# One row of loads and one woven stretch for the first two expert units

## The reference, cut to what matters

```python
logits = (x @ w_router).astype(jnp.float32)
top_v, top_i = lax.top_k(logits, TOP_K)              # 2 of 8 experts for each token
gates = jax.nn.softmax(top_v, axis=-1)
combine = jnp.sum(jax.nn.one_hot(top_i, N_EXPERTS) * gates[..., None], axis=1)
for e in range(N_EXPERTS):
    out = out + combine[:, e:e + 1] * _swiglu(x, w_gate[e], w_up[e], w_down[e])
```

## Time and profile before

| | |
|---|---|
| Median of 3 runs | 1327.22 us (1326.99 to 1327.36) |
| The profiled execution | 1327.16 us, its span 1325.4 us |
| PE, DVE, ACT busy | 1279.3, 795.5, 642.1 us |
| Bytes moved, mean rate | 425.55 MB, 321 GB/s over the span |
| Issues on SP's queue | 422.67 MB |

### The profile page before, as it was taken

The page is one execution under the profiler, slowest core; times in us unless marked ns, Lnnn a source line. Parts: engine busy times, 40 slices in busy tenths (PEclk is TensorE's granted clock), DMA queues, the critical chain, the costliest instruction groups (busy, mean ns, idle before and its releaser), DMA issues.

```text
span 1325.4 us, 19510 instructions
## 1 busy us (share of the span) xinstructions
PE 1279.3 (97%) x7976; PEld 985.7 (74%) x7976; DVE 795.5 (60%) x977; ACT 642.1 (48%) x675; POOL 4.5 (0%) x12
## 2 busy tenths in 40 slices
PE   8999999999999999999769999999999999999996
PEld 8999999999999977885448885347887345888332
DVE  7564765653888679973129883118886215888122
ACT  7655644352576586761037772017774005776002
POOL 0000000000000000000000000000000000000000
PEclk9999999999999999999889999999999999999998
DMA  7335354463333498899999999999999999999995
GB/s 300 134 128 190 128 191 159 159 221 138 116 144 128 163 383 325 338 385 400 426 426 426 426 427 427 427 398 427 427 426 427 427 406 425 427 427 427 426 427 231
DMA packets 72351, 425.55 MB, mean 321 GB/s; under 512 B 6385, under 2 KB 8433, under 8 KB 27329
## 3 DMA queue, kind: packets, MB, share of 16 engines
q1 hardware_dynamic: 71680, 422.67, 78.6%
q0 software_dynamic: 432, 1.54, 0.3%
q10 hardware_dynamic: 144, 0.02, 0.0%
HBM read 423.16 MB, written 1.05 MB: 320 GB/s over the span
## 4 chain that ended last, share of the span: by engine, by line
PE 81%; DVE 8%; DMA 5%; ACT 3%; issue 3%; SPq 0%; DVEq 0%; ACTq 0%
PE ps L2436 11%; PE ps L2297 8%; PE ps L2298 7%; PE ps L2303 7%; PE ps L2468 6%; PE ps L1752 5%; PE ps L1742 4%; PE ps L1743 4%; PE ps L2322 4%; PE ps L2323 4%; PE ps L2330 4%; DMA unsplit<-in_moe_w_up 2%; PE ps L1790 2%; PE ps L1791 2%; PE ps L1807 2%
## 5 line engine op out<-in xcount | busy, mean ns | idle before, releaser
L1402 DVE TENSOR_TENSOR wl<-raw,wh 128x2048 fp32r<-128x2048 f32 x96 | 218.4, 2288 | 23.7 <-ACT wh L866 23.6
L866 ACT CAST wh<-raw 128x2048 fp32r<-128x2048 f32 x96 | 183.9, 1916 | 66.1 <-PE ps L2298 39.3
L2297 PE MATMUL ps<-wh,gh 128*128 128x512 f32 x448 | 176.3, 394 | 4.1 <-ACT wh L866 3.4
L2298 PE MATMUL ps<-wh,gl 128*128 128x512 f32 x448 | 175.4, 392 | 0.0
L937 ACT ACTIVATE sil<-ps 64x512 f32<-64x512 f32 (+1 forms) x28 | 15.0, 536 | 291.3 <-PE ps L2438 225.1
L2303 PE MATMUL ps<-wl,gh 128*128 128x512 f32 x448 | 120.4, 391 | 0.0
L1626 DVE COPY few_act<-ps 128x256 f32<-128x256 f32 (+1 forms) x28 | 11.0, 391 | 175.2 <-PE ps L2450 175.2
L1066 DVE TENSOR_TENSOR wl<-raw,wh 128x4096 fp32r<-128x4096 f32 (+1 forms) x18 | 73.2, 4069 | 61.7 <-ACT wh L625 39.7
L625 ACT CAST wh<-raw 128x4096 fp32r<-128x4096 f32 (+2 forms) x29 | 92.0, 3173 | 34.5 <-PE ps L1743 34.1
L2297 PEld LDWEIGHTS ps<-wh,gh 128*128 128x128 f32 x448 | 84.6, 189 | 23.9 <-issue 5.5
L2303 PEld LDWEIGHTS ps<-wl,gh 128*128 128x128 f32 x448 | 84.6, 189 | 17.9 <-DVE wl L1402 0.2
(11 more groups left out here) (365 smaller groups left out, 2672.0 us busy)
## 6 DMA issues: line engine op xcount, KB each, us to landing
raw<-in_moe_w_up SPq DMA_DIRECT2D x71, 1024.0 KB, 14.2
raw<-in_moe_w_gate SPq DMA_DIRECT2D x70, 1024.0 KB, 12.9
raw<-in_moe_w_down SPq DMA_DIRECT2D x51, 1024.0 KB, 14.5
unsplit<-in_moe_w_down SPq DMA_DIRECT2D x33, 1024.0 KB, 11.9
unsplit<-in_moe_w_up SPq DMA_DIRECT2D x25, 1024.0 KB, 14.4
unsplit<-in_moe_w_gate SPq DMA_DIRECT2D x22, 1024.0 KB, 19.1
raw_more<-in_moe_w_down SPq DMA_DIRECT2D x15, 1024.0 KB, 12.0
raw<-in_diff_w_qkv SPq DMA_DIRECT2D x8, 1536.0 KB, 6.6
```

The source lines that it names most:

```text
L866: act.copy(split_piece(wh, p), raw_piece(p, first)).then_inc(wh_ready, 1)
L1402: dve.tensor_tensor(split_piece(wl, p), raw_piece(p, first), raw_f(split_piece(wh, p)), ALU.subtract).then_inc(wl_ready, 1)
L2297: pe.matmul(ps[:, bank, :], gh[:, s], w, start=(k0 + k == 0), stop=False)
L2298: ins = pe.matmul(ps[:, bank, :], gl[:, s], w, start=False, stop=False)
```

## The change

1. The loads of the first wide unit and of the tiny unit become one list (`first_pair`) of 84 pieces. Place q mod 11 is taken by entry q, so both share eleven places and the six lent ones are not used in this pair. The list begins with 24 wide pieces; then come 4 tiny, 6 wide, 6 tiny, 6 wide, 6 tiny, 6 wide, and then the other 26 tiny ones.
2. PE weaves: after chunk i of the wide unit, for i = 3 to 6, it runs one share of the tiny unit (`tiny_share(i - 3)`): the transposition of the tiny chunk before, gate and up of the tiny chunk, down of the one before. The last three tiny chunks follow the wide unit (`tiny_rest`).
3. The tiny unit gets banks 5 (gate and up) and 6 (down) and buffers in `xn`; `gather` for the next unit goes to banks 0 and 1, both halves after chunk 5.
4. The routing on DVE is earlier: sort at j = 0, count at 1, list at 2, `save_tokens(3)` at j = 3 (it was at 1), `pick_pair(0)` at 5. PE's `gather_few(0)` and `turn_picks(0)` come after chunk 2. `turn(0)` waits for three saved tiles, and `down` of chunk 0 for the fourth.
5. `gather_few(1)` and `turn_picks(1)` come after the loop of `tiny_rest`, before the last two tiny down pieces.

```diff
+        def few_share(t):
+            return [("few", p) for p in range(few_up_at(t), few_up_at(t) + (6 if t else 4))]
+        def first_pair():
+            chunk = [CPU * 2 * c // FC - 2 if c else 0 for c in range(FC)] + [PIECES - 2, PIECES]
+            order = [("wide", p) for p in range(chunk[TINY_LAG])]
+            for t in range(FC - TINY_LAG):
+                order += [("wide", p) for p in range(chunk[t + TINY_LAG] + (2 if t else 0), chunk[t + TINY_LAG + 1] + 2)]
+                order += few_share(t)
+            for t in range(FC - TINY_LAG, FC):
+                order += few_share(t)
+            return order + [("few", p) for p in range(PIECES - 2, PIECES)]
...
+            def load_pair():
+                e = 0
+                for q, (kind, p) in enumerate(pair):
+                    s = q % RAW_SLOTS
+                    if q >= RAW_SLOTS:
+                        before, of = pair[q - RAW_SLOTS]
+                        if before == "wide":
+                            sp.wait_ge(wl_ready, C_MOE + of + 1)
+                        else:
+                            sp.wait_ge(few_used, of + 1)
...
+                    if p == 0:
+                        sp.wait_ge(routed, 1)
+                        e = expert(SMALL_UNITS[0])
...
-            load_wide(0, 0, first=True)
-            sp.wait_ge(routed, 1)
+            load_pair()
```

On ACT:

```diff
+            def tiny_rest():
+                for i in range(FC - TINY_LAG, FC):
+                    few_silu(0, i)
+                    if i == 5:
+                        gathered_high(2, unit=1)
+                few_tokens(1)
+                turned_picks(1)
...
                 for j, (kind, i) in enumerate(unit_chunks):
+                    if first and (kind, i) == ("g", TINY_LAG):
+                        few_tokens(0)
+                        turned_picks(0)
+                    if first and kind == "g" and i > TINY_LAG:
+                        few_silu(0, i - TINY_LAG - 1)
```

On DVE:

```diff
+            def tiny_rest():
+                wide_out(0)
+                few_turned_out(0, FC - TINY_LAG - 1)
+                dve.wait_ge(pick_turned, 1)
+                pick_pair(2)
+                dve.memset(bm["y"][:], 0.0)
+                for i in range(FC - TINY_LAG, FC):
+                    few_product(0, i)
+                    if i < FC - 1:
+                        add_wide(0, i - (FC - TINY_LAG))
+                    few_turned_out(0, i)
+                    if i == 5:
+                        gathered_low(2, unit=1)
...
+                    if first and kind == "g" and i > TINY_LAG:
+                        few_product(0, i - TINY_LAG - 1)
...
+                    if first and kind == "d" and TINY_LAG <= i < FC - 1:
+                        few_turned_out(0, i - TINY_LAG)
                     if 2 * j + 4 < PIECES:
                         unit_split(a, 2 * j + 4, first)
-                    if first and j < 2:
-                        save_tokens(2 + j)
+                    if first and j == 0:
+                        save_tokens(2)
+                        sort_experts()
+                    if first and j == 1:
+                        count_units()
                     if first and j == 2:
-                        sort_experts()
+                        list_units()
                     if first and j == 3:
-                        count_units()
-                    if first and j == 4:
-                        list_units()
+                        save_tokens(3)
+                    if first and j == 5:
+                        dve.wait_ge(gathered, 2)
+                        pick_pair(0)
...
-                    if first and j == 9:
-                        dve.wait_ge(gathered, 2)
-                        pick_pair(0)
```

On PE:

```diff
+            def few_turn(f, i):
+                pe.wait_ge(few_prod, f * FC + i + 1)
+                if i:
+                    pe.wait_ge(few_act_ready, f * FC + i)
+                if f == TINY_AT:
+                    pe.wait_ge(eal_ready, min(i + TINY_LAG + 2, FC))
...
+            def tiny_share(t):
+                if t:
+                    few_turn(0, t - 1)
+                few_up(0, t, 0)
+                few_up(0, t, 1)
+                if t:
+                    few_down(0, t - 1, 0)
+                    few_down(0, t - 1, 1)
+            def tiny_rest():
+                for i in range(FC - TINY_LAG, FC):
+                    few_up(0, i, 0)
+                    few_turn(0, i - 1)
+                    few_up(0, i, 1)
+                    few_down(0, i - 1, 0)
...
+                    if i in (4, 5):
+                        scatter_wide(0, i - 4)
+                    if i == 5:
+                        pe.wait_ge(pick_of, 2)
+                        gather(0, 1)
+                        gather(1, 1)
+                gather_few(1)
+                turn_picks(1)
+                few_down(0, FC - 1, 0)
+                few_down(0, FC - 1, 1)
...
                     pe.wait_ge(eal_ready, a * FC + i + 1)
+                    if first and i == 0:
+                        pe.wait_ge(acc_ev, 4)
...
                     elif first:
-                        pe.wait_ge(acc_ev, 4)
+                        pe.wait_ge(acc_ev, 3)
+                    if first and i > TINY_LAG + 1:
+                        pe.wait_ge(few_act_ready, i - TINY_LAG - 1)
...
-                    if first and i == 5:
+                    if first and i == TINY_LAG - 1:
                         gather_few(0)
                         turn_picks(0)
+                    if first and i >= TINY_LAG:
+                        tiny_share(i - TINY_LAG)
```

More of the change, by code:

```diff
@@ L528, in load_wide @@
+            def load_wide(a, e, few=None):
+                for p, (s, n) in enumerate(WIDE_PLACES):
                     kind, i = unit_chunks[p // 2]
                     if n:
[L531 to L542, removed]
+                        sp.wait_ge(wl_ready, a * PIECES + C_MOE + last_at(WIDE_PLACES[:p], s) + 1)
@@ L995, in _ @@
                 output_out(f)
-                few_body(u, f)
+                if f:
+                    few_body(u, f)
+                else:
+                    tiny_rest()
                 if u < LAST:
@@ new lines, in few_turn @@
+            def few_turn(f, i):
+                pe.wait_ge(few_prod, f * FC + i + 1)
+                if i:
+                    pe.wait_ge(few_act_ready, f * FC + i)
+                if f == TINY_AT:
+                    pe.wait_ge(eal_ready, min(i + TINY_LAG + 2, FC))
+                for k in range(few_cols(f) // P):
+                    s = slice(k * P, (k + 1) * P)
+                    ins = pe.transpose(ps[:, 4, s], few_prod_of(f)[:, s], ident)
+                ins.then_inc(few_turned, 1)
@@ new lines, in few_down @@
+            def few_down(f, i, half):
+                p = few_down_at(i) + half
+                if half == 0:
+                    pe.wait_ge(few_act_ready, f * FC + i + 1)
+                    if i == 0 and f:
+                        pe.wait_ge(wide_low, 2 * f + 2)
+                pe.wait_ge(*few_in(f + 1, f, p))
+                for k in range(2):
+                    held_, n = held(f), few_cols(f)
+                    to = slice((half * 2 + k) * held_, (half * 2 + k + 1) * held_)
+                    first_, last_ = i == 0 and half == 0 and k == 0, i == FC - 1 and half == 1 and k == 1
+                    for h in range(D // n):
+                        s = slice(k * D + h * n, k * D + (h + 1) * n)
+                        ins = pe.matmul(ps[h * held_:(h + 1) * held_, few_out_bank(f), 0:n], bm["few_act"][:, i % 2, to],
+                                        few_piece(f, p)[:, s], start=first_, stop=last_, skip_group_check=True)
+                ins.then_inc(few_used, 1)
@@ new lines, in few_body @@
+            def few_body(u, f):
+                few_up(f, 0, 0)
+                few_up(f, 0, 1)
+                for i in range(1, FC):
+                    few_up(f, i, 0)
+                    few_turn(f, i - 1)
+                    few_up(f, i, 1)
+                    few_down(f, i - 1, 0)
+                    if i == FC - 1:
+                        few_turn(f, i)
+                    few_down(f, i - 1, 1)
+                    before_ = 8 * f - 4
+                    if i in (1, 2):
+                        scatter_wide(f, i - 1)
+                    if i in (3, 4):
+                        scatter_few(f - 1, i - 3, (3, 7), before_ + 2 + 2 * (i - 3))
+                    if u < LAST and i in (3, 4):
+                        if i == 3:
+                            pe.wait_ge(pick_of, f + 2)
+                        gather(i - 3)
+                    if u < LAST and i == 5:
+                        gather_few(f + 1)
+                    if u < LAST and i == 6:
+                        turn_picks(f + 1)
+                few_down(f, FC - 1, 0)
+                few_down(f, FC - 1, 1)
```

252 lines of the change are left out of this document (126 added, 126 removed).

## The result

The changed kernel takes 1330.03 us (median of 14 runs, 1329.12 to 1331.25) against 1327.51 us (14 runs on the same chips, 1325.82 to 1329.69): ratio 1.0019, 95% interval 1.0011 to 1.0027, so 2.5 us slower. The forecast was 1328.5. The profiled execution took 1330.08 us with a span of 1328.2, 2.9 more than the one before.

A forecast was written before the change was run, and what follows sets the result against it. Weight transfers were taken to bound the kernel from slice 19 (630 us). Recovered idle transfers -6.7 plus a dense stream starting 8.0 us late gave +1.3 us, 1328.5; the forecast's own range was 1325.5 to 1332.

The forecast's parts named there:

- What bounds: Transfers bound from slice 19 (630 us); the landing of load 85, about 686, sets the next wide unit's start.
- Joining the lists: Loads of both units: tiny pieces fill SP's waits, the stream is dense from load 35 on, 6.7 us come back.
- The late saved tile: PE before down of chunk 0: stands still from 503.3 to 512.3, 9 us, waiting for DVE's last saved tile.
- The clock: PE behind the 9 us wait: slow clock costs 2.3 us; bounds 0 and 4.6 if two pieces run slow.
- PE dense from 512 on, SP's issues: First wide unit: piece 21 used at 557.9, loads 33 to 35 issued at 554.7, 557.5, 559.7; dense stream 8.0 us late.
- The woven stretch costs nothing: Shares among wide chunks: no cost if the stream stays fed; tightest at share 1, with three loads under way, 7.4 us.
- Rival C: Woven shares: PE waits 5.0 us a share for silu, product, cast and subtraction; 4.3 us paid, 1332.8; chance 0.17.
- A, filling alone: Dense stream's start: no PE wait, load 35 about 1 us late, idle transfers recovered, 1321.5; chance 0.18.
- B, the clock staying up: PE behind the saved-tile wait: the wait is there but no slow clock, -1.0 us, 1326.2; chance 0.15.
- `gather_few(1)` in the tail: End of tiny unit: gather, picks and two down pieces done at 687.3 against PE's next start at 689.3, two microseconds of cover.

The follow-up runs named there:

- filled gap: Changed kernel plus 20 unread matmuls of 256 columns on PE before the wait for the fourth saved tile: 1326.92 us, ratio 0.9993.
- lead of two: Two wide pieces loaded ahead of each share's tiny ones; taken out of the kernel with the routing at its old steps: 1339.84 us, ratio 1.0085.
- the kernel without the lead and with the turned tile first: Kernel without the two-wide-piece lead, with ACT and DVE taking the turned tile out ahead of piece 2j+3 in d3 to d5: 1332.53 us, ratio 1.0042.

## Why the prediction was right, and where its sizes were off

The experiments make a path from the kernel before to the changed one: gather early +2.5, row and weave -7.5, early routing +1.2, late saved tile +6.4 (1.0019 against 0.9971). They are differences of ratios, each uncertain by about 2 us, and they add up to the measured 2.5 by construction, so the sum proves nothing. On another path the parts would differ: the stall at turn 2 that goes with the early gather is not in the changed kernel, whose turn 2 starts at 534.31 without a wait.

The time was forecast at +1.3 and measured at +2.5. The terms were -6.7 + 8.0 and measured -6.4 + 10.3 = +3.9 at load 85. That the time is closer to the forecast than this is luck: the microsecond that comes back between load 85 and the end of the span (3.9 there, 2.9 here), most of it near 880, stands nowhere in the prediction, and no experiment was made on it.

*What bounds.* Right. The next wide unit is started by a transfer in both traces, 3.5 us later in the changed kernel, and the added PE work at share 2 cost nothing.

*Joining the lists.* Right in size: 6.7 forecast, 6.4 come back. The prediction gave all of it to the joined lists, though; with the gather early and the lists as before, 2.6 of them had come back already.

*The late saved tile.* Right: PE idle from 503.3 to 512.3 forecast, 8.78 us ending at 512.60 measured, released by DVE's copy, with DVE full meanwhile. Taking the wait away gave 5.6 us and adding it to the kernel before cost 5.4 by the ratio. The claim that the transfers would not hide what reaches load 35 held.

*The clock.* The mechanism was right; the term was mis-sized. I took 2.3 us, one slow piece. The spell that I forecast was there, from the gap to 517. A second one stood at 541 to 544, while piece 16 ran behind the small matmuls of the gather; this I did not have. The filled gap measured 3.1 to 3.4 us for both. That is 0.8 to 1.1 us above the term; with 0.3 us of later start at piece 8 it is about half of the 2.5 us by which turn 3 ran at 557.3 and not at 554.8. A wait of 0.41 us at that turn is another part, and the rest is not split. By the same 2.5 us load 35 landed at 566.5 and not at 564.

*PE dense from 512 on, SP's issues.* Right in kind; 33 and 34 were issued 2 us later than the sum had them, behind the same delay of PE.

*The woven stretch costs nothing.* Right for this order of loads: 425 from 586 on. My reason was only half the reason. I argued from the three loads under way and the three split pieces that lie ready, and by that argument the lead of two should not have mattered. It was worth 16.7 us. Rival C named the coupling of ACT's order with the shares, but priced it at 5 us a share and took silu and product for its carrier; what carries it, once the lead is gone, is the turned tile in bank 4 behind casts that wait for transfers.

*Rivals.* A, filling alone, was false for this kernel, and its condition is real: with the tile early the time was 1324.4. That is still 2.9 above A's 1321.5, for load 35 was 4.9 us late (561.1 for 556.2) where A had 1. With the routing back at its old steps and the gather and the gates moved as well, it was 1317.2, below A's figure, for PE's own stalls go too. The rule of the Trainium skill (Perfetto Trace Analysis, Optimization Strategy), that interleaving regimes with different limits may pay, is borne out here by the 7.5 us for row and weave; what the change moved on DVE beside it cost more. B, the clock staying up, was false, but the filled gap gave 1326.9 where B said 1326.2.

*`gather_few(1)` in the tail.* The last down pieces ended at 690.5, PE's next start was 692.8: covered, with 2.3 us to spare (2.0 forecast).

## What to carry to other kernels

When two stages are woven, list for each engine what it does in order between taking in one stage's data and freeing what the other stage needs; each load that such an engine takes ahead of the release must be ahead in the load queue as well. Small steps moved about on a full engine are priced by who waits behind them: the same 0.7 us copy two steps later, with PE's wait for it, made the kernel before 5.4 us slower. Ask of each delay how much of it reaches the point from which transfers bound the rest: the 8.8 us of idle PE made load 35 later by 5.4 (566.5, for 561.1 with the tile early), and about that much was paid. Behind that point 4 us of PE work were free where PE had to wait for its data anyway; so move what nobody needs yet (here the gates) behind it.

## What the runs showed of the hardware that was not expected

Unread matmuls in a gap of 8.8 us made the kernel 3.1 us faster: the granted clock stayed at 2.4 GHz where it had been 1.2 GHz from 507 to 517 and again from 541 to 544. The spell at 541 had no idle time ahead of it: PE was busy for all of 517 to 541, at the end with 32 small matmuls of the gather. Shorter waits were enough as well: 2.64 us at turn 2 in the kernel with the routing at its old steps, with a half clock from 527.3 to 530.7. Which of such gaps brings a slow spell stayed open. The wait of 2.25 us at turn 3, in the kernel with the gather after chunk 3, had none, and the same 2.64 us at turn 2, in the kernel without the lead and with the turned tile first, had none either:

```profile
526.44 0.66 PE L2628 MATMUL ps<-base,act 128*128 128x128 f32 x4 [2.64 <-DVE act L1788]
```

```profile
527.00:530.70 3.70, 3.70 (x23) 3.21 (x23) 3.56 (x7) 2.27 (x2) 0.00 (x0) 1.00 1.02 432
```

So the length of a wait alone does not tell whether the clock falls.
